# Putting the first key indices of four tokens on one partition: one 512-column product per group in the expert gather of a two-layer decoder

## What is computed

```
q   = x @ w_q                       8 heads, two halves of 128
s1  = q1 @ k1, s2 = q2 @ k2         128 keys each; top 16 of both
c   = s1[top] + s2[top]             16 x 16 candidates; top 16
row = i1 * 128 + i2                 of 16384 experts, 128 per token (8 heads x 16)
h   = gelu(x . u[row])
out = sum over the 128 rows of softmax(c) * h * v[row]
```

## Time and profile before

| | |
|---|---|
| timed runs (3) | 2261.77, 2264.06, 2265.73 us; median 2264.06 us |
| span of the profiled execution | 2353.7 us |
| profiled span over the median | 2353.7 - 2264.06 = 89.6 us longer; what lies around the span is not shown for this execution |
| TensorE busy | 2044.5 us, 87% |
| DVE, ACT, POOL busy | 1177.2 us, 650.0 us, 1001.2 us |
| moved by DMA | 529.91 MB, mean 225 GB/s |
| dense passes | 360 to 725 us, and 1555 to 1918 us |
| groups | 725 to 1175 us, and 1918 to 2353 us |

### The profile page before, as it was taken

One profiled execution on the slowest core, in us unless ns is written; L12 is line 12 of the kernel. 1 busy time (PEld: TensorE's weight loads), 2 busy tenths in 40 slices (PEclk: granted clock), 3 DMA queues, 4 the chain that ended last, 5 costly groups with the idle time before them and its releaser, 6 DMA issues.

```text
span 2353.7 us, 38380 instructions
## 1 busy us (share of the span) xinstructions
PE 2044.5 (87%) x14289; PEld 1496.2 (64%) x14289; DVE 1177.2 (50%) x3447; ACT 650.0 (28%) x977; POOL 1001.2 (43%) x874
## 2 busy tenths in 40 slices
PE   9889999999997667889898889999999986777777
PEld 4554899999995323334356346999999973233332
DVE  2554699423333533578456834997233333333333
ACT  1332244545551001112134022454555520000000
POOL 0111469830004565656514303688500026666665
PEclk9899999999998798999997989999999998888878
DMA  6473434444447999999932334244444469999998
GB/s 233 173 279 119 144 129 159 161 162 162 168 163 264 331 355 369 362 329 335 350 122 62 90 116 152 81 161 153 162 168 164 165 217 348 360 346 357 365 357 312
DMA packets 179914, 529.91 MB, mean 225 GB/s; under 512 B 22066, under 2 KB 49234, under 8 KB 179474
## 3 DMA queue, kind: packets, MB, share of 16 engines
q0 software_dynamic: 87296, 310.68, 36.3%
q1 hardware_dynamic: 91282, 216.25, 26.8%
q10 hardware_dynamic: 1152, 0.52, 0.1%
HBM read 524.69 MB, written 2.69 MB: 224 GB/s over the span
## 4 chain that ended last, share of the span: by engine, by line
PE 68%; another core or an unknown queue 8%; DVE 8%; POOL 5%; issue 5%; DMA 3%; ACT 2%; SPq 1%; DVEq 0%; ACTq 0%; PEldq 0%
PE bank L950 10%; PE bank L952 10%; PE bank L951 10%; PE bank L769 8%; PE bank L1014 8%; PE bank L990 4%; POOL u_low L703 3%; PE bank L1032 3%; PE bank L1092 2%; DVE i_one_hot L2172 2%; DMA v_slot<-in_peer_v,v_rows 2%; POOL v_slot L712 2%; PE bank L979 1%; PE bank L1242 1%
## 5 line engine op out<-in xcount | busy, mean ns | idle before, releaser
L712 POOL DMA_INDIRECT v_slot<-in_peer_v,v_rows x417 | 394.6, 946 | 703.8 <-PE bank L952 441.1
L950 PE MATMUL bank<-h_parts,u_high 128*128 128x288 f32 x2048 | 607.0, 296 | 7.9 <-POOL u_low L703 6.2
L951 PE MATMUL bank<-h_parts,u_high 128*128 128x288 f32 x2048 | 604.4, 295 | 0.0
L952 PE MATMUL bank<-h_parts,u_low 128*128 128x288 f32 x2048 | 602.8, 294 | 0.0
L950 PEld LDWEIGHTS bank<-h_parts,u_high 128*128 128x128 f32 x2048 | 384.1, 188 | 11.6 <-POOL u_low L703 9.6
L952 PEld LDWEIGHTS bank<-h_parts,u_low 128*128 128x128 f32 x2048 | 385.8, 188 | 0.0
L951 PEld LDWEIGHTS bank<-h_parts,u_high 128*128 128x128 f32 x2048 | 384.6, 188 | 0.0
L1597 ACT CAST u_high<-u_slot 128x1024 fp32r<-128x1024 f32 x256 | 268.7, 1050 | 400.5 <-PE bank L952 249.1
L703 POOL TENSOR_TENSOR u_low<-u_slot,u_high 128x1024 fp32r<-128x1024 f32 x120 | 321.1, 2686 | 93.5 <-ACT u_high L1597 93.4
L1014 PE MATMUL bank<-v_slot,weight_columns 128*32 128x512 f32 x1412 | 274.1, 687 | 57.3 <-DMA v_slot<-in_peer_v,v_rows 34.1
L1014 PE MATMUL bank<-v_slot_of_columns,weight_columns 128*32 128x512 f32 x636 | 246.2, 687 | 69.8 <-DVE weight_columns L2179 44.0
(11 more groups left out here) (393 smaller groups left out, 2463.2 us busy)
## 6 DMA issues: line engine op xcount, KB each, us to landing
u_slot<-in_peer_ut SPq DMA_DIRECT2D x256, 512.0 KB, 3.5
w_q<-in_peer_w_q SPq DMA_DIRECT2D x8, 2048.0 KB, 14.4
region<-in_cache_a_kt SPq DMA_DIRECT2D x8, 960.0 KB, 11.8
region<-in_cache_a_v SPq DMA_DIRECT2D x8, 960.0 KB, 11.4
v_slot<-in_peer_v,v_rows POOLq DMA_INDIRECT x417
region<-in_ev_w_in SPq DMA_DIRECT2D x3, 2048.0 KB, 15.1
region<-in_pool_kv POOLq DMA_DIRECT2D x40, 128.0 KB, 5.0
ckv_t_norm<-in_pool_ckv SPq DMA_DIRECT2D x64, 64.0 KB
```

Source lines behind the costliest of these rows:

```text
L712: pool.indirect_dma_start(out=VS[l][slot], out_offset=None, in_=v_rows, in_offset=bass.IndirectOffsetOnAxis(ap=IDX[:, at:at + 1], axis=0)) ...
L950: pe.matmul(bank, uh, HR[:, 0, c, :], start=(c == 0), stop=False)
L951: pe.matmul(bank, uh, HR[:, 1, c, :], start=False, stop=False)
L952: ins = pe.matmul(bank, ul, HR[:, 0, c, :], start=False, stop=(c == KC - 1))
```

## The change

The i1 values of a group's four tokens are put side by side on one partition, once per tile, during the dense pass. `turn_route(t)` gets a second bank: four products whose stationary operand is every fourth column of the identity (from column i) put the i1 values of token 4j + i on partition j, in columns 128i to 128i + 127. DVE copies that bank to `I1G` in bf16; tile 0 lies on partitions 0 to 31, tile 1 on 32 to 63, the sample groups on 64 to 71. `spread_i1(q)` is then one product of 512 columns with a stationary operand of 32 (or 8) partitions. The copies that wrote I1B for t = 0 and 1 go; I1B for t = 2 stays, under another name and in another place.

```diff
-        I1B = tile_at("i1_tokens", [3, P], HT_AT + D, BF16)
-        I2T = tile_at("i2_pairs", [NT], HT_AT + D + 192)
-        GT = tile_at("gate_pairs", [NT], HT_AT + D + 480)
-        IDX = tile_at("v_rows", [NT], HT_AT + D + 768, U32)
-        ROWF = tile_at("v_rows_f", [P], HT_AT + D + 1056)
+        I1G = tile_at("i1_of_groups", [4, P], HT_AT + D, BF16)
+        I2T = tile_at("i2_pairs", [NT], HT_AT + D + 256)
+        GT = tile_at("gate_pairs", [NT], HT_AT + D + 544)
+        IDX = tile_at("v_rows", [NT], HT_AT + D + 832, U32)
+        ROWF = tile_at("v_rows_f", [P], HT_AT + D + 1120)
+        I1B = tile_at("i1_sample_tokens", [P], HB[2] + 5120, BF16)
+
+        def group_rows(t):
+
+            return slice(64, 72) if t == 2 else slice(32 * t, 32 * t + 32)
...
                     ins.then_inc(d_full, 1)
+                    bank = to_dve()
+                    for i in range(4):
+                        out = bank[group_rows(t), i * P:i * P + P]
+                        if t < 2:
+                            ins = pe.matmul(out, ident[:, i:P:4], ROUTE[:, t, 0, :], start=True, stop=True)
+                        else:
+                            ins = pe.matmul(out, ident32[:, i:NS:4], I1B, start=True, stop=True)
+                    ins.then_inc(d_full, 1)
...
-                    for i in range(4):
-                        out = banks[q % 2][:, i * P:i * P + P]
-                        at = ident32[:, 4 * j + i:4 * j + i + 1] if kind == "sample" else ident16[:, 4 * j + i:4 * j + i + 1]
-                        ins = pe.matmul(out, at.broadcast_to([P, P]), I1B[:, 2 if kind == "sample" else kind, :], start=True, stop=True)
-                    ins.then_inc(sem("i1_spread"), 1)
+                    R = group_rows(2 if kind == "sample" else kind)
+                    pe.matmul(banks[q % 2][:, :], ident16[R, R.start + j:R.start + j + 1].broadcast_to([R.stop - R.start, P]),
+                              I1G[R].rearrange("p i k -> p (i k)"), start=True, stop=True).then_inc(sem("i1_spread"), 1)
...
-                    if t < 2:
-                        link(dve.tensor_copy(I1B[:, t, :], ROUTE[:, t, 0, :]))
-                    else:
-                        link(dve.memset(I1B[:, t, :], 0.0))
+                    if t == 2:
+                        link(dve.memset(I1B, 0.0))
                         for c in range(4):
                             R = slice(NS * c, NS * c + NS)
-                            link(dve.tensor_copy(I1B[R, t, 32 * c:32 * c + 32], ROUTE[R, t, 0, 0:2 * TOPK]))
+                            link(dve.tensor_copy(I1B[R, 32 * c:32 * c + 32], ROUTE[R, t, 0, 0:2 * TOPK]))
...
                     TS(IDX[:, a:a + rows], ROWF[:, 0:rows], float(l * NK * NK), None, ALU.add)
+                    bank = full()
+                    R = group_rows(t)
+                    link(dve.tensor_copy(I1G[R].rearrange("p i k -> p (i k)"), bank[R, :]))
+                    free()
```

## The result

The changed kernel takes 2270.9 us (median of 10 runs, 2268.73 to 2275.93) beside 2265.67 us of the kernel before on the same chip (10 runs, 2261.77 to 2272.09): a ratio of 1.0025, 95% interval 1.0013 to 1.0037. It is slower by 5.2 us, a little more than this kernel's measurement can tell from nothing. The forecast was 2253.3 us, 10.8 us faster. The time lies inside the stated range, but it moved the other way than was forecast: it is the rival "nothing in the groups", 2266 to 2269 us, and slightly more.

What follows compares the result with a forecast made beforehand. TensorE was taken to bound the dense pass and 105 groups, DMA the other groups. Span 2353.7 - 15.8 (spread) + 5.0 (added work) = 2342.9 us; against the runs' median 2264.06 - 10.8 = 2253.3 us, range 2230 to 2274.

Steps and rivals of the forecast that it cites:

- nothing in the groups: Rival, chance 0.31: DMA bounds the groups or the loads were already hidden; only added work remains, 2266 to 2269 us.
- TensorE's real work sets the pace of a group: Second stage of groups and first from about 900 us: TensorE works through a queue and paces 105 groups.
- The ceiling of the prediction: Second stage: DMA's fastest 50 us, 376 GB/s, lets a group shrink from 5.92 to 5.62 us, room for 0.30.
- as it is: Whole run: the profiled span's 89.6 us above the runs' median carried over unchanged, 2264.06 - 10.8 = 2253.3 us.
- The term of the spread: Groups: one spread product for four saves 0.15 us on each of 105 groups, 15.8 us.
- The lower bound from the earlier trace: Spread: products start 0.056 us apart with loads hidden, four costing 0.22 us like one of 512 columns; saving nothing.
- the load and a half: Spread: of three weight loads of 0.105 us, one and a half taken as exposed, 0.15 us per group.
- The added turn: Dense pass, TensorE: added products for I1G plus a bank wait cost 2.5 us per layer, 5.0 in all, not hidden.
- wait for a bank: Dense pass: TensorE waits for DVE to free banks in the turn, 0 to 1.5 us per layer, 0.5 taken.
- DVE at nothing: Dense pass, DVE: two 2.33 us copies per layer go, three of some 0.8 us come; no effect on time.
- More than a load and a half: Rival, chance 0.20: each spread product pays its own load, 0.30 us per group, 31.5 us less 5: 2237.6 us.
- The clock: Rival: TensorE's clock in the groups falls oftener to 1.2 GHz, slower, 2275 us mild; chance 0.14 including longer bank wait.

Runs made afterwards that it cites:

- one_product: Kernel before with one spread product of 128 columns per group in place of four, except in each layer's first two groups: 2263.96 us, 0.9988.
- twice: Kernel before with each of the four 128-column spread products made two times per group: 2266.55 us, 0.9999.
- dma_turn: Changed kernel with the prompt tiles' I1G filled by eight small DMAs per layer in place of TensorE's products: 2266.77 us, 0.9999 of the kernel before.
- after: The changed kernel itself, in its first profile: 2270.9 us, 1.0025 of the kernel before.
- after_again: The changed kernel unchanged, run and profiled a second time: 2272.84 us, 1.0027 of the kernel before.
- turn_only: Kernel before with the added products and copies that make I1G, which nothing reads; spread left at four products: 2272.02 us, 1.0024.
- the pair with half rows: Kernel before gathering 2 KB rows: 2214.21 us, 0.9778; the same with one 512-column spread product, I1G filled with ones: 2215.5 us, 0.9779.

## Why the prediction was wrong

**The failed step: "TensorE's real work sets the pace of a group".** The prediction put this at 105 of the 144 groups. The runs show DMA in its place: in the second profile of the same kernel TensorE waits 105.4 us of 300 for rows of v, DMA stands at 409 GB/s, POOL has no "remote" waits in that stretch, and half the bytes take 31.5 and 21.4 us off the two stages. The step rested on late releases in one profiled execution. The ceiling of the prediction, 376 GB/s from the fastest 50 us, was the speed of that execution, not the most that DMA reaches. The prediction named this as its weakest step. The evidence that it was weak lay in the times: a span 4% above every timed run, when all that was to be costed sat in two stages of it. Carrying the 89.6 us over "as it is" took them for a constant; they were 40.9 and 52.9 us of the two stages, 0.6 and 0.7 us of each group, far more than the 0.15 under discussion.

Two more marks of that execution could be read. Its page gives no time to landing for the gathers, and the second profile's does:

```profile
v_slot<-in_peer_v,v_rows POOLq DMA_INDIRECT x417
```

```profile
v_slot<-in_peer_v,v_rows POOLq DMA_INDIRECT x417, 8.2
```

Counted in the traces themselves, the first one holds 3949 of the 9216 landing signals of the 576 gathers (16 each), and the other thirteen traces hold 9179 to 9206. Where landings are not recorded, a wait can hardly be put down to them, so the 6.2 us of the earlier trace rows are no measure of how long TensorE waited for rows. And its DMA engines were busy 0.97 of the time for 357 GB/s, where they were busy 1.03 for 409 afterwards: 8% more busy time per byte. This points to slower DMA in that execution. Its cause stays open, and so does why the releases came late in it; no second profile shows either.

**The term of the spread, 0.15 us a group on 105 groups.** It was wrong twice. It was covered (`one_product`, `twice` and `dma_turn`: nothing that can be told from zero), and there was hardly anything to be covered: DVE is served 0.42 us after the start in the median, and 0.44 before, 0.02 us of the 0.15. The lower bound from the earlier trace rows was the truth; the load and a half was chosen against a row that showed no exposed load. With the one product the first `pick` even starts later after it, 0.32 us against 0.24.

Of the two rules weighed in the prediction, the one with the small saving was right. The 0.43 against 0.44 us agree with the single-product rule of the Trainium skill's page "TensorE: Matmul & The Clock Gate", section "Back-to-back issue gap" (four of 128 columns 222 ns, one of 512 216 ns). Its stream rule of 81 ns at 128 columns did not hold here: four more products moved DVE's start by 0.22 us, 55 ns each.

**The added turn, 2.5 us per layer.** Right in kind, and too large by the wait. 16 fp32 records took 2 x 1.02 = 2.04 us (predicted 1.8), the bf16 ones up to 0.39 (0.2), and no wait for a bank shows between the tiles, only 0.17 us of "issue" (0.5 taken, 0 to 1.5 bounded). Block 3.6 us, predicted 3.5. The dense passes last 413.2 us on the mean over the eight profiles without a turn (16 passes, 412.6 to 413.8) and 415.0 over the three with it (`after`, `after_again`, `turn_only`: 6 passes, 413.7 to 416.3): 1.8 us per layer, 3.6 in all. By the interval of the first result the whole change costs 2.9 to 8.4 us, so the 1.6 us between 3.6 and its median of 5.2 are within the noise.

**DVE at nothing.** Right. The new copies took 0.68 us (0.8 predicted). The two copies of 2.33 us that went brought nothing: DVE's wait of 28.36 us for the turned routes, which lies behind them, is 28.36 us in the kernel after, too.

**The rivals.** "Nothing in the groups" is what happened, and its argument, "the same 512 columns, and a DMA that is nearly full", was both halves of the truth. It had a chance of 0.31, hardly less than the forecast's 0.35. "More than a load and a half" falls with the term. The clock hardly moved with this change and cost nothing: see below.

## What to carry to other kernels

Hold the span of a profile against the timed runs before you cost anything from it: where it is some per cent longer, find out which stage holds the surplus, and take no bound, no rate and no wait from that stage before a second profile confirms them. A page that lists gathers without a time to landing is a second warning: it lacks the records by which waits are put down to DMA. Fewer instructions with the same columns gained nothing on TensorE, since the loads already hid; a row that shows them hidden outweighs an argument that they might not be. And work that is moved out of a covered stage into one where its engine is full costs most of its length, however small the saving on the other side is: 1.8 of 2.5 us per layer here, for nothing.

## What was not expected of the hardware

**The granted clock went with the number of small products.** From 1930 to 2180 us, `twice` (eight products of 128 columns a group), `one_product` (one) and `dma_turn` (one of 512, on 32 rows) had, in this order:

```profile
1930.00:2180.00 250.00, 168.04 (x1525) 90.11 (x1527) 101.99 (x484) 0.00 (x0) 185.66 (x199) 0.98 1.03 409
```

```profile
1930.00:2180.00 250.00, 184.18 (x1206) 83.31 (x1204) 101.41 (x483) 0.00 (x0) 184.37 (x197) 0.84 1.03 409
```

```profile
1930.00:2180.00 250.00, 185.90 (x1205) 79.00 (x1205) 102.19 (x486) 0.00 (x0) 184.82 (x198) 0.90 1.03 409
```

TensorE's busy time is longer at the lower clock, with fewer records. A window of one profile can mislead, so the timed runs are the better witness; their granted clock over the whole kernel was 0.957 to 0.966 in 12 runs of `twice`, 0.933 to 0.943 in 12 of `one_product`, and 0.945 to 0.957 in the 23 of the kernel before beside them. The three ranges meet only at 0.957. The change itself, with 512 columns before and after, hardly moved it: 0.945 to 0.952 in 12 runs of `after_again` (mean 0.949), 0.943 to 0.957 in the 17 of the kernel before beside them (mean 0.951). So leaving out three of the four products did go with a lower clock, which is in kind what the rival said, and the change's one product of 512 columns did not, to any extent. The lower clock cost nothing that shows: GB/s was 409 in this stretch at 0.84 as at 0.98, and TensorE had some 100 us of 300 of waiting for rows to spend. In the pair with half rows the clocks were alike, 0.94 and 0.93, and so were the times.

**Two walls close together.** DMA's 5.13 us a group for rows of 4 KB and POOL's 4.98 for four indirect issues lie 3% apart: halving the bytes of the gather brought 2.2 to 2.4% of the time, 31.5 us in the first stage and 21.4 in the second (profile against profile), and no more.
